# Gathered rows split into down and up halves, with five and seven places of their own, in a decoder layer with a product-key FFN

## The chip, the cores and the metric

The program runs on one core of a Trainium2 chip, in one launch. The metric is the device time of that core in microseconds. The engines are TensorE (PE), VectorE (DVE), ScalarE (ACT), GpSimd (POOL) and SyncE (SP, which only issues transfers); they run beside each other and meet at semaphores. Sixteen DMA engines move data between the chip's DRAM and the on-chip memory of 128 partitions.

## What is computed

One decoder layer on 1024 tokens of width 1024. A mixer (causal pooling, and spatial gating by chunks of 128 tokens) adds to x. Then each token picks 16 of 16,384 experts in each of 8 heads, and a weighted sum of the experts' rows adds to x again. The second part, cut down:

```python
q = (xb @ w_query).reshape(T, 8, 2, 128)
scores = jnp.einsum('thpd,hpkd->thpk', q, sub_keys)      # 128 keys each
s_top, i_top = lax.top_k(scores, 16)
cand = s_top[:, :, 0, :, None] + s_top[:, :, 1, None, :]
cand_idx = i_top[:, :, 0, :, None] * 128 + i_top[:, :, 1, None, :]
best, sel = lax.top_k(cand.reshape(T, 8, 256), 16)
idx = jnp.take_along_axis(cand_idx.reshape(T, 8, 256), sel, axis=-1)
gate = jax.nn.softmax(best, axis=-1)
u_e, v_e = expert_down[idx], expert_up[idx]              # 1024 floats each
act = jax.nn.gelu(jnp.einsum('thkd,td->thk', u_e, xb))
out = jnp.einsum('thk,thkd->td', gate * act, v_e)
```

So each of the 1024 tokens reads 128 down rows and 128 up rows of 4 KB, 1.07 GB in all, all in float32.

## The kernel before

The tokens are eight tiles of 128. The experts of a tile are served in 128 **slots**; slot g = 0 to 1023 runs over all tiles (`TABLE`, made by `slot_table`). A slot is one gather for 128 partitions, each with a token and one chosen expert: an indirect DMA that GpSimd issues, with a row of 8 KB for each partition from the table `experts`, in which an expert's down row and up row lie side by side. It moves 1 MB.

What happens to slot g, in this order:

- **L581**, POOL: the gather into place `x.ring`. Up to g = 267 there are 6 places of 8 KB (`RING_MIX`), from g = 268 (`LATE_SLOT`) 8. It waits until PE has used the row that was in the place before (`s_free`).
- **L1324**, DVE, `dot(x)`: waits for the row (`s_row`), multiplies the down half with the token's vector and sums it; the products overwrite the down half.
- **L950, L952, L957**, ACT, `expert_weight(x)`: gelu, times the gate, and a matrix `diag` of 128 x 32 that carries the weight.
- **L768**, PE, `add_expert(x)`: four matmuls (eight instructions in the trace, since float32 takes two passes) that add diag x up half into PSUM; the last one raises `s_free`.

Every engine has its program written out by hand as a loop over `TABLE`; after the work of slot g it does what else is due at g. The mixer of tile 1 to 7 is cut into 35 steps, and step n of tile t is due at slot `MIX_AT[t]` + n; the last is at slot 264. PE's share of these steps is the matmuls of L629, L640, L649, L659, L667 and L685. Routing (the choice of experts) for two heads at a time has its steps at `ROUTE_AT`: matmuls L737 and L750 on PE, 19 small steps on DVE. A slot's matmul therefore stands in PE's queue behind the mixer and routing matmuls of the slots before. Each engine works through its queue in order, and POOL issues slot g before slot g + 1.

Memory on chip is full. While the mixers run, `weights` holds w_in and w_out (20 units of 4 KB a partition), and `work` holds the 6 places, two buffers for the routing weights (`side_buf`) and the spread token vectors. After the last mixer step 16 routing blocks (`sides`, 576 KB each, 4.6 KB a partition) are loaded into `weights` for good, and two more places become free: one behind them, and one in `side_buf`. Before slot 0 two places hold the first routing blocks.

## Time and profile before

| | us |
|---|---|
| median of 3 runs | 2921.01 (2916.40 to 2921.32) |
| the profiled execution | 2921.73 |
| its span, first to last instruction | 2919.7 |

| engine | busy us | share of the span |
|---|---|---|
| PE matmul | 1976.8 | 68% |
| DVE | 1913.9 | 66% |
| ACT | 1210.3 | 41% |
| POOL | 1131.4 | 39% |

The DMA engines moved 1170.03 MB at a mean of 401 GB/s. The queue of the gathers alone held 147,456 packets and 1073.81 MB: 144 packets a gather, 128 rows and 16 that only signal. All other transfers are 93.84 MB. No compute engine is near its whole time, and the transfers are at 90% of it, so the table is to be read by stages: a stage has its own bound, and the mean over all hides it.

### The profile page before, as it was taken

How to read it: one execution, taken by the hardware profiler on the slowest of the kernel's cores; microseconds unless marked ns; L12 is line 12 of the kernel's file. 1: busy time of each engine (PE TensorE's matmuls, PEld its weight loads, DVE VectorE, ACT ScalarE, POOL GpSimd, SP SyncE). 2: the span in 40 equal slices, each digit the busy share in tenths (PEclk: the TensorE clock that was granted, in tenths of full speed). 3: DMA queues.
4: the chain of work that ended last, by engine and by line, in shares of the span. 5: the costliest groups of instructions: out<-in, count | busy, mean ns of one | idle time of the engine just before them, and what ended most of it. 6: DMA issues, size and time to landing. Idle time of an engine off the chain costs nothing.

```text
span 2919.7 us, 37542 instructions
## 1 busy us (share of the span) xinstructions
PE 1976.8 (68%) x12772; PEld 903.1 (31%) x12772; DVE 1913.9 (66%) x4710; ACT 1210.3 (41%) x3859; POOL 1131.4 (39%) x1032
## 2 busy tenths in 40 slices
PE   5788887887878566666666666566666666666554
PEld 4454443543534222222222323232222223232110
DVE  4876757665766376667576766667576766666554
ACT  1245444354544244444344444444344444444333
POOL 0044334344333344444444444444444444444332
PEclk9889988989889556666666656666666656565555
DMA  9599999999999999999999999999999999999997
GB/s 405 203 366 400 371 381 401 378 420 375 420 420 380 418 378 421 421 409 421 421 421 421 408 417 421 420 407 420 421 418 416 409 410 419 421 401 420 420 421 312
DMA packets 173396, 1170.03 MB, mean 401 GB/s; under 512 B 19475, under 2 KB 28691, under 8 KB 39958
## 3 DMA queue, kind: packets, MB, share of 16 engines
q0 software_dynamic: 147456, 1073.81, 89.9%
q1 hardware_dynamic: 25750, 93.84, 8.2%
q8 instruction: 101, 1.65, 0.2%
q14 instruction: 89, 0.73, 0.1%
HBM read 1159.18 MB, written 8.39 MB: 400 GB/s over the span
## 4 chain that ended last, share of the span: by engine, by line
DMA 50%; PE 24%; DVE 12%; ACT 7%; issue 3%; SPq 2%; POOL 1%; DVEq 0%; POOLq 0%; ACTq 0%
DMA work<-experts,expert_rows 42%; PE ps_sum L768 8%; DMA weights<-experts,expert_rows 6%; DVE work L1324 5%; PE ps_small L737 4%; PE ps_m L685 4%; PE ps_wide L711 3%; PE ps_m L649 2%; ACT diag L957 2%; PE ps_m L629 2%; ACT weight L952 2%; DMA out<-h_next 1%; SPq L543 1%; ACT act_out L950 1%; PE ps_m L640 1%
## 5 line engine op out<-in xcount | busy, mean ns | idle before, releaser
L581 POOL DMA_INDIRECT work<-experts,expert_rows x930 | 1027.6, 1105 | 1618.8 <-PE ps_sum L768 1438.2
L1324 DVE CUSTOM_DVE_ANT_0 work<-work 128x1024 f32<-128x1024 f32 x930 | 1134.5, 1222 | 720.1 <-DMA work<-experts,expert_rows 718.5
L768 PE MATMUL ps_sum<-work,diag 128*32 128x256 f32 x7440 | 837.4, 535 | 769.6 <-ACT diag L957 766.3
L950 ACT ACTIVATE act_out<-act_in 128x1 f32<-128x1 f32 x1024 | 207.5, 203 | 1189.4 <-DVE act_in L1324 1186.4
L768 PEld LDWEIGHTS ps_sum<-work,diag 128*32 128x32 f32 x7440 | 171.9, 127 | 1301.3 <-ACT diag L957 1228.1
L957 ACT ACTIVATE diag<-const,weight 128x32 f32<-128x32 f32 x1024 | 329.1, 321 | 33.5
L952 ACT ACTIVATE weight<-gate,act_out 128x1 f32<-128x1 f32 x1024 | 301.6, 295 | 33.2
L737 PE MATMUL ps_small<-h_t,weights 128*128 128x128 f32 x1344 | 299.5, 392 | 0.0
L737 PEld LDWEIGHTS ps_small<-h_t,weights 128*128 128x128 f32 x1344 | 257.0, 286 | 132.3 <-issue 125.0
L711 PE MATMUL ps_wide<-h_cur,const 32*128 32x512 f32 x260 | 209.4, 896 | 0.8 <-ACT work L924 0.8
L768 PE MATMUL ps_sum<-weights,diag 128*32 128x256 f32 x752 | 88.4, 557 | 108.0 <-ACT diag L957 100.9
L1324 DVE CUSTOM_DVE_ANT_0 weights<-weights,work 128x1024 f32<-128x1024 f32 x94 | 115.0, 1224 | 70.5 <-DMA weights<-experts,expert_rows 70.4
L581 POOL DMA_INDIRECT weights<-experts,expert_rows x94 | 100.8, 1072 | 142.3 <-PE ps_sum L768 140.4
L924 ACT COPY work<-ps_wide 128x512 f32<-128x512 f32 x144 | 83.6, 581 | 133.4 <-PE ps_wide L711 125.6
L685 PE MATMUL ps_m<-weights,h_buf 128*128 128x512 f32 x256 | 126.6, 621 | 0.7 <-DVE h_buf L1193 0.7
L737 PE MATMUL ps_small<-h_t,work 128*128 128x128 f32 x640 | 101.7, 310 | 0.9 <-ACT wide L937 0.9
L737 PEld LDWEIGHTS ps_small<-h_t,work 128*128 128x128 f32 x640 | 91.3, 218 | 35.3 <-issue 34.0
L931 ACT COPY q_t<-ps_small 128x128 f32<-128x128 f32 x124 | 32.4, 261 | 138.2 <-PE ps_small L737 137.4
L1324 DVE DVE_READ_ACCUMULATOR2_ANT act_in<- 128x1 f32 x1024 | 83.6, 82 | 0.0
L711 PEld LDWEIGHTS ps_wide<-h_cur,const 32*128 32x128 f32 x260 | 52.2, 249 | 82.3 <-issue 80.4
L950 ACT ACT_TABLE_LOAD x59 | 75.7, 1283 | 2.8 <-DVE act_in L1324 1.8
L649 PE MATMUL ps_m<-h_t,weights 128*128 128x128 f32 x512 | 76.2, 297 | 0.0
(161 smaller groups left out, 1665.8 us busy)
## 6 DMA issues: line engine op xcount, KB each, us to landing
work<-sides SPq DMA_DIRECT2D x44, 576.0 KB, 8.1
work<-w_ada SPq DMA_DIRECT2D x12, 2048.0 KB, 23.5
work<-experts,expert_rows POOLq DMA_INDIRECT x930, 16.2
weights<-sides SPq DMA_DIRECT2D x16, 576.0 KB, 37.2
weights<-w_in SPq DMA_DIRECT2D x3, 2048.0 KB, 17.5
x_buf<-x SPq DMA_DIRECT2D x8, 512.0 KB, 11.2
weights<-w_out SPq DMA_DIRECT2D x2, 2048.0 KB, 35.9
x_scratch<-h_buf SPq DMA_DIRECT2D x8, 512.0 KB, 8.1
```

The costliest lines, as they stand in the source:

```text
L581: nc.gpsimd.indirect_dma_start(ring[x.ring], None, experts, bass.IndirectOffsetOnAxis(ap=rows_flat[:, x.column:x.column + 1], axis=0),).th ...
L629: last = nc.tensor.matmul(ps_v[:, :], h_t[:, k, :], w_in_sb[:, 0, k, :], start=(k == 0), stop=(k == KC - 1))
L649: last = nc.tensor.matmul(ps_u[:, g * P:(g + 1) * P], w_in_sb[:, 2, k, g * P:(g + 1) * P], h_t[:, k, :], start=(k == 0), stop=(k == KC - 1))
L685: last = nc.tensor.matmul(ps_out[half], mixed_t[:, k, :], w_out_sb[:, k, half * HALF:(half + 1) * HALF], start=(part == 0 and i == 0), sto ...
L711: nc.tensor.matmul(ps_wide[:, :], quads[quarter(group), :], source[quarter(group), half * HALF:(half + 1) * HALF], start=True, stop=True). ...
L737: last = nc.tensor.matmul(ps_query(n), w_q[:, k, :], h2_t[:, k, :], start=(k == 0), stop=(k == KC - 1))
L768: last = nc.tensor.matmul(ps_sum[quarter(c), x.group, :], diag[:, x.ring, :], ring[x.ring][:, D + c * QCOLS:D + (c + 1) * QCOLS], start=x. ...
L924: nc.scalar.copy(h2_spread[k % 2][:, half * HALF:(half + 1) * HALF], ps_wide[:, :]).then_inc(s_wide_sb, 1)
L950: nc.scalar.activation(act_out[:, s:s + 1], act_in[:, s:s + 1], ACT.Gelu).then_inc(s_gelu, 1)
L952: nc.scalar.mul(weight[:, s:s + 1], gate_flat[:, x.column:x.column + 1], act_out[:, s:s + 1]).then_inc(s_weight, 1)
L957: nc.scalar.mul(diag[:, x.ring, :], quad_rows, weight[:, s:s + 1]).then_inc(s_diag, 1)
L1324: nc.vector.tensor_tensor_reduce(down, down, h2_spread[x.segment % 2], 1.0, 0.0, ALU.mult, ALU.add, act_in[:, x.g % TURN:x.g % TURN + 1]). ...
```

## The change

Up to slot 267 a slot is two gathers in place of one: 4 KB a partition from a table `downs`, and 4 KB from a table `ups`. Both tables are further inputs. The 12 half places of the six old places are the same memory (`UP_PLACES`, `DOWN_PLACES`), now five for down rows and seven for up rows. A down place is free when the dot of its last row is done (`s_dots`), an up place when PE has used its last row (`s_free`). POOL issues down g, up g, down g + 1 and so on. The dot waits for the down row alone; PE's product waits for the up row too. From slot 268 on whole rows go from `experts` into eight pairs of places, as before. `diag` has eight matrices throughout, no longer numbered by the ring. `weights` and `work` become parts of one tensor, `arena`.

```diff
 
 
-RING_MIX = 6
-RING = 8
+
+
+UP_PLACES = (20, 21, 22, 23, 24, 25, 26)
+DOWN_PLACES = (27, 31, 28, 29, 30)
+LATE_PAIRS = (18, 32, 20, 22, 24, 26, 28, 30)
+ALL_PLACES = range(18, 34)
+FIRST_SIDE_PLACE, SIDE_PLACE = 28, 32
+DIAGS = 8
 MIX_TILES = 2
 LATE_SLOT = 268
-LATE_ORDER = (6, 7, 4, 5, 0, 1, 2, 3)
 
 
...
         self.tile, self.s = g // SLOTS, g % SLOTS
-        self.ring = g % RING_MIX if g < LATE_SLOT else LATE_ORDER[g % RING]
-        self.fill, self.before = 0, None
+        self.up = self.down = self.up_before = self.down_before = None
+        self.down_fill = self.up_fill = 0
+        self.diag, self.whole = g % DIAGS, False
         self.first = self.last = self.opens = False
 
...
                         table.append(x)
-    fills, last = [0] * RING, [None] * RING
+    fills = dict.fromkeys(ALL_PLACES, 0)
+    last = {place: None for place in ALL_PLACES}
+
+    def longest_free(choices, halves):
+        def last_use(place):
+            return max(-1 if last[place + i] is None else last[place + i][1] for i in range(halves))
+        return min(choices, key=last_use)
+
     for x in table:
-        fills[x.ring] += 1
-        x.fill, x.before = fills[x.ring], last[x.ring]
-        last[x.ring] = x.g
+        x.whole = x.g >= LATE_SLOT
+        if x.whole:
+            x.down = longest_free(LATE_PAIRS, 2)
+            x.up = x.down + 1
+        else:
+            x.down, x.up = longest_free(DOWN_PLACES, 1), longest_free(UP_PLACES, 1)
+        x.down_before, x.up_before = last[x.down], last[x.up]
+        last[x.down], last[x.up] = ("free" if x.whole else "dot", x.g), ("free", x.g)
+        for place in {x.down, x.up} if not x.whole else {x.down}:
+            fills[place] += 1
+        x.down_fill, x.up_fill = fills[x.down], fills[x.up]
     return table, starts
 
 
 TABLE, SEGMENTS = slot_table()
 
 
-FIRST_SIDES = {2: 4, 3: 5}
+FIRST_SIDES = (2, 3)
 
...
 
-        weights = sb("weights", [P, KC * (IN_WIDTH + D)])
+        arena = sb("arena", [P, KC * (IN_WIDTH + D) + 12 * D + 2 * SIDE + 2 * D])
+        weights = arena[:, 0:KC * (IN_WIDTH + D)]
+        places = arena[:, 0:36 * D].rearrange("p (h n) -> p h n", n=D)
         w_in_sb = weights[:, 0:KC * IN_WIDTH].rearrange("p (b k n) -> p b k n", b=3, k=KC)
         w_out_sb = weights[:, KC * IN_WIDTH:].rearrange("p (k n) -> p k n", k=KC)
...
+
+        work = arena[:, KC * (IN_WIDTH + D):]
         ada_stage = [work[:, i * KC * D:(i + 1) * KC * D].rearrange("p (k n) -> p k n", k=KC) for i in range(2)]
-        ring = [work[:, r * 2 * D:(r + 1) * 2 * D] for r in range(RING_MIX)]
-        at_sides = RING_MIX * 2 * D
-        ring += [weights[:, SIDES * SIDE:SIDES * SIDE + 2 * D], work[:, at_sides:at_sides + 2 * D]]
-        side_buf = [work[:, at_sides + i * SIDE:at_sides + (i + 1) * SIDE] for i in range(2)]
-        at_spread = at_sides + 2 * SIDE
+        first_side_buf = {b: arena[:, FIRST_SIDE_PLACE * D + i * SIDE:FIRST_SIDE_PLACE * D + (i + 1) * SIDE]
+                          for i, b in enumerate(FIRST_SIDES)}
+        at_sides = SIDE_PLACE * D
+        side_buf = [arena[:, at_sides + i * SIDE:at_sides + (i + 1) * SIDE] for i in range(2)]
+        at_spread = 12 * D + 2 * SIDE
         h2_spread = [work[:, at_spread + i * D:at_spread + (i + 1) * D] for i in range(2)]
 
...
@@ -567,21 +591,33 @@
             for row in (gate1, shift2, scale2):
                 nc.gpsimd.memset(row[:, :], 0.0).then_inc(s_zero, 1)
             pool.wait_ge(s_acc, N_MOD * KC)
+
+            def both_places(x):
+                return arena[:, x.down * D:(x.down + 2) * D]
+
+            def wait_free(place, before):
+
+                if before is not None:
+                    pool.wait_ge(s_dots if before[0] == "dot" else s_free, before[1] + 1)
+                elif place >= SIDE_PLACE:
+                    pool.wait_ge(s_score, 4 * HELD_FROM)
+                elif FIRST_SIDE_PLACE <= place < FIRST_SIDE_PLACE + 3:
+                    pool.wait_ge(s_score, 4)
+
             for x in TABLE:
                 if x.opens:
                     pool.wait_ge(s_placed, x.tile * PAIRS + x.batch[-1] + 1)
                 if x.g == LATE_SLOT:
                     pool.wait_ge(s_o, TILES)
-                if x.before is not None:
-                    pool.wait_ge(s_free, x.before + 1)
-                elif x.ring == RING - 1:
-                    pool.wait_ge(s_score, 4 * HELD_FROM)
-                elif x.ring in FIRST_SIDES.values():
-                    pool.wait_ge(s_score, 4)
-                nc.gpsimd.indirect_dma_start(
-                    ring[x.ring], None, experts,
-                    bass.IndirectOffsetOnAxis(ap=rows_flat[:, x.column:x.column + 1], axis=0),
-                ).then_inc(s_row[x.ring], 16)
+                offset = bass.IndirectOffsetOnAxis(ap=rows_flat[:, x.column:x.column + 1], axis=0)
+                wait_free(x.down, x.down_before)
+                if x.whole:
+                    wait_free(x.up, x.up_before)
+                    nc.gpsimd.indirect_dma_start(both_places(x), None, experts, offset).then_inc(s_row[x.down], 16)
+                    continue
+                nc.gpsimd.indirect_dma_start(places[:, x.down, :], None, downs, offset).then_inc(s_row[x.down], 16)
+                wait_free(x.up, x.up_before)
+                nc.gpsimd.indirect_dma_start(places[:, x.up, :], None, ups, offset).then_inc(s_row[x.up], 16)
 
 
...
@@ -764,9 +800,11 @@
                 if x.g == 0:
                     pe.wait_ge(s_gate2, 1)
                 pe.wait_ge(s_diag, x.g + 1)
+                if not x.whole:
+                    pe.wait_ge(s_row[x.up], 16 * x.up_fill)
                 for c in range(QUADS):
-                    last = nc.tensor.matmul(ps_sum[quarter(c), x.group, :], diag[:, x.ring, :],
-                                            ring[x.ring][:, D + c * QCOLS:D + (c + 1) * QCOLS],
+                    last = nc.tensor.matmul(ps_sum[quarter(c), x.group, :], diag[:, x.diag, :],
+                                            places[:, x.up, c * QCOLS:(c + 1) * QCOLS],
                                             start=x.first, stop=x.last, skip_group_check=True)
                 last.then_inc(s_free, 1)
...
@@ -952,9 +990,9 @@
                 nc.scalar.mul(weight[:, s:s + 1], gate_flat[:, x.column:x.column + 1],
                               act_out[:, s:s + 1]).then_inc(s_weight, 1)
                 act.wait_ge(s_weight, x.g + 1)
-                if x.before is not None:
-                    act.wait_ge(s_free, x.before + 1)
-                nc.scalar.mul(diag[:, x.ring, :], quad_rows, weight[:, s:s + 1]).then_inc(s_diag, 1)
+                if x.g >= DIAGS:
+                    act.wait_ge(s_free, x.g - DIAGS + 1)
+                nc.scalar.mul(diag[:, x.diag, :], quad_rows, weight[:, s:s + 1]).then_inc(s_diag, 1)
 
             def square3(n):
...
@@ -1317,10 +1355,10 @@
                 nc.vector.tensor_copy(gate[:, :, columns], moved[:, 1, :, :]).then_inc(s_wide_sb, 1)
 
             def dot(x):
-                dve.wait_ge(s_row[x.ring], 16 * x.fill)
+                dve.wait_ge(s_row[x.down], 16 * x.down_fill)
                 if x.g == SEGMENTS[x.segment][0]:
                     dve.wait_ge(s_wide_sb, WIDE_USE["copy", x.segment, 1] + 1)
-                down = ring[x.ring][:, 0:D]
+                down = places[:, x.down, :]
                 nc.vector.tensor_tensor_reduce(down, down, h2_spread[x.segment % 2], 1.0, 0.0, ALU.mult, ALU.add,
                                                act_in[:, x.g % TURN:x.g % TURN + 1]).then_inc(s_dots, 1)
...
         "experts": np.concatenate([np.asarray(expert_down)[0], np.asarray(expert_up)[0]], axis=1),
+        "downs": rows(np.asarray(expert_down)[0]), "ups": rows(np.asarray(expert_up)[0]),
         "g_final": rows(g_final).reshape(-1),
         "constants": shape_constants(), "first_constants": first_tile_constants(),
```

On **GpSimd**, before slot 0 and the slots behind it, the kernel before:

```order
L581 DMA work<-experts,expert_rows 128x2048 [waits choices_placed,ada_sum_steps]
L581 DMA work<-experts,expert_rows 128x2048 x3
L581 DMA work<-experts,expert_rows 128x2048 [waits side_score_psum_ready] x2
L581 DMA work<-experts,expert_rows 128x2048 [waits ring_slots_used] x26
L581 DMA work<-experts,expert_rows 128x2048 [waits ring_slots_used,choices_placed]
```

and the changed one, from slot 4 to slot 7 (`dots_ready` is `s_dots`, `ring_slots_used` is `s_free`):

```order
L618 DMA arena<-downs,expert_rows 128x1024 [waits side_score_psum_ready]
L620 DMA arena<-ups,expert_rows 128x1024
L618 DMA arena<-downs,expert_rows 128x1024 [waits dots_ready]
L620 DMA arena<-ups,expert_rows 128x1024
L618 DMA arena<-downs,expert_rows 128x1024 [waits dots_ready]
L620 DMA arena<-ups,expert_rows 128x1024
L618 DMA arena<-downs,expert_rows 128x1024 [waits dots_ready]
L620 DMA arena<-ups,expert_rows 128x1024 [waits ring_slots_used]
```

Slot 6 was the first to wait for PE; now down 5 is the first that waits for a dot, and up 7 the first that waits for PE. In all 268 instructions more stand in this queue.

On **PE**, in the mixer of tile 1 (L649 is a projection of the mixer, L659 the spatial product; L685 and L695 are their numbers after), the kernel before:

```order
L659 MATMUL ps_m<-w_sp_t,vn_u 128x128 x3
L768 MATMUL ps_sum<-work,diag 32x256 [waits diags_ready]
L768 MATMUL ps_sum<-work,diag 32x256 x3
L649 MATMUL ps_m<-h_t,weights 128x128 x4
L768 MATMUL ps_sum<-work,diag 32x256 [waits diags_ready]
```

and the changed one:

```order
L695 MATMUL ps_m<-w_sp_t,vn_u 128x128 x3
L806 MATMUL ps_sum<-arena,diag 32x256 [waits rows_in_place26_landed,diags_ready]
L806 MATMUL ps_sum<-arena,diag 32x256 x3
L685 MATMUL ps_m<-h_t,arena 128x128 x4
L806 MATMUL ps_sum<-arena,diag 32x256 [waits rows_in_place20_landed,diags_ready]
```

Nothing moved on PE; the first matmul of a product waits for one more semaphore. The other engines' queues keep their order.

## Rows read from the trace of the kernel before

**Rows 1.** Stages: length, busy us of each engine (instructions), PE clock, DMA share, GB/s

```profile
148.00:944.00 796.00, 655.24 (x4372) 351.53 (x4371) 536.12 (x1408) 370.50 (x1107) 308.89 (x269) 0.88 0.99 393
944.00:1040.00 96.00, 43.37 (x250) 20.25 (x250) 38.69 (x79) 27.43 (x84) 26.77 (x26) 0.55 0.97 398
1040.00:2900.00 1860.00, 1179.14 (x7698) 466.00 (x7698) 1236.82 (x3049) 779.47 (x2593) 792.73 (x729) 0.62 1.01 416
```

**Rows 2.** The same view: a late stretch, and two saturated ones among the mixers

```profile
1110.00:1280.00 170.00, 111.80 (x732) 48.20 (x732) 114.28 (x286) 68.84 (x236) 72.90 (x68) 0.64 1.01 421
...
590.00:660.00 70.00, 57.72 (x380) 30.76 (x378) 46.39 (x127) 40.21 (x114) 29.09 (x24) 0.83 1.02 420
740.00:870.00 130.00, 106.16 (x718) 53.53 (x715) 93.00 (x257) 62.30 (x189) 52.24 (x48) 0.88 1.01 420
```

**Rows 3.** The same view: six stretches in which PE is nearly always busy

```profile
210.00:230.00 20.00, 20.00 (x96) 8.51 (x96) 6.63 (x14) 6.58 (x23) 6.28 (x6) 0.95 0.90 340
330.00:360.00 30.00, 28.39 (x152) 12.41 (x151) 17.62 (x43) 11.67 (x37) 10.03 (x9) 0.97 0.90 323
400.00:440.00 40.00, 36.81 (x291) 26.28 (x292) 24.05 (x61) 18.00 (x51) 13.87 (x12) 0.96 0.93 346
530.00:550.00 20.00, 19.74 (x170) 13.65 (x169) 8.79 (x13) 6.84 (x24) 8.46 (x7) 1.00 0.85 329
690.00:720.00 30.00, 28.58 (x174) 13.01 (x173) 14.52 (x26) 10.40 (x39) 12.02 (x10) 1.00 0.93 343
870.00:900.00 30.00, 29.07 (x261) 21.85 (x260) 14.77 (x29) 13.85 (x43) 11.99 (x11) 1.00 0.97 376
```

**Rows 4.** Line L581, 148 to 944 us: issues, POOL's waits, who waits for them

```profile
L581 POOL DMA_INDIRECT work<-experts,expert_rows x269: 933/938/2529, 148.1 to 940.1; - x135
...
  PE ps_sum L768: 473.8, 247
...
  DVE work L1324: 149.1, 112
```

**Rows 5.** Timeline at 412 us: start, us, engine, line, operation, idle time before

```profile
412.16 1.22 DVE L1324 CUSTOM_DVE_ANT_0 work<-work 128x1024 f32<-128x1024 f32 x1
413.41 1.22 DVE L1324 CUSTOM_DVE_ANT_0 work<-work 128x1024 f32<-128x1024 f32 x1
419.89 0.64 PE L768 MATMUL ps_sum<-work,diag 128*32 128x256 f32 x8
420.83 0.94 POOL L581 DMA_INDIRECT work<-experts,expert_rows  x1 [2.86 <-PE ps_sum L768]
428.65 1.23 DVE L1324 CUSTOM_DVE_ANT_0 work<-work 128x1024 f32<-128x1024 f32 x1 [2.66 <-DMA work<-experts,expert_rows]
```

**Rows 6.** Timeline of POOL: three of the first six issues

```profile
148.07 1.08 POOL L581 DMA_INDIRECT work<-experts,expert_rows  x1 [144.52 <-DVE expert_rows L1316]
149.46 0.94 POOL L581 DMA_INDIRECT work<-experts,expert_rows  x1 [0.30 <-issue]
...
151.94 0.93 POOL L581 DMA_INDIRECT work<-experts,expert_rows  x1 [0.31 <-issue]
```

**Rows 7.** Timeline at 339 us: a dot and two issues

```profile
339.22 1.23 DVE L1324 CUSTOM_DVE_ANT_0 work<-work 128x1024 f32<-128x1024 f32 x1 [0.97 <-DMA work<-experts,expert_rows]
...
339.27 1.99 POOL L581 DMA_INDIRECT work<-experts,expert_rows  x1 [3.27 <-PE ps_sum L768]
...
341.56 1.05 POOL L581 DMA_INDIRECT work<-experts,expert_rows  x1 [0.30 <-issue]
```

**Rows 8.** Stretches: 16 KB rows; 16 side loads beside gathers; single loads beside gathers

```profile
30.00:62.00 32.00, 23.44 (x114) 17.00 (x114) 14.58 (x21) 3.23 (x10) 0.00 (x0) 0.95 1.01 431
...
950.00:970.00 20.00, 6.53 (x45) 2.21 (x46) 10.71 (x23) 6.89 (x18) 9.37 (x10) 0.50 1.02 419
...
720.00:730.00 10.00, 4.43 (x37) 2.12 (x36) 3.34 (x5) 1.79 (x7) 4.45 (x5) 0.88 1.02 428
```

**Rows 9.** Line L768, 148 to 944 us: what ended PE's idle time before it

```profile
  ACT diag L957: 337.6, 199
```

More of the change, by code:

```diff
@@ L392, in build @@
         s_h2c = sem("h2_cur_ready")
-        s_row = [sem(f"expert_row{r}_landed") for r in range(RING)]
+        s_row = {place: sem(f"rows_in_place{place}_landed") for place in ALL_PLACES}
         s_free = sem("ring_slots_used")
@@ L520, in _ @@
             for b in range(2, 4):
[L521 removed]
+                sp.dma_start(first_side_buf[b], sides[b]).then_inc(s_side0, 16)
             load_x(1)
```

8 lines of the change are left out of this document (3 added, 5 removed).

## The prediction

> **What bounds the kernel now.** I read the table of stages first, because one share over the whole span hides two different kernels [rows 1]. Up to 148 us nothing is gathered. From 1040 us to 2900 us the DMA engines move 416 GB/s at a share of 1.01: they are the bound there, and the change leaves that part's transfers as they are. Between 148 and 944 us, while the mixers run, they move only 393 GB/s. The 796 us at 393 GB/s are 312.8 MB; at the 421 GB/s of an undisturbed late stretch [rows 2] they would take 743 us. So 53 us is all that this stage could give back if nothing else moved. That stage holds the 268 gathers that the change splits: the first starts at 148.07 us [rows 6], the 269th at 940.1 us [rows 4], so a row now takes (940.1 - 148.1) / 268 = 2.96 us.
>
> Where are the 53 us? The second table of stretches shows six in which PE is busy 92 to 100% of the time and the DMA falls to 323 to 376 GB/s [rows 3]. Against 421 GB/s they lose 20 x 81 + 30 x 98 + 40 x 75 + 20 x 92 + 30 x 78 + 30 x 45 = 13,090, over 421: 31 us. In the saturated stretches between them the rate is 420 GB/s and there is nothing to gain [rows 2]. The rest of the 53 us is spread thin, part of it in transfers with 1 KB rows.
>
> Who holds the gathers up there? GpSimd (POOL) issues them, and in this stage it waits 473.8 us, 247 times, for PE's expert product L768, which empties a place [rows 4]. One loop of such a stretch stands in [rows 5]: PE ends the product at 419.89 + 0.64 = 420.53 us, POOL issues into the emptied place at 420.83 us, and that row's dot on VectorE starts at 428.65 us, after 2.66 us of idle time put down to the DMA. The product itself is late because PE has mixer matmuls in front of it, not because its row is late: the dot that ended at 412.16 + 1.22 = 413.38 us belongs to the product of 420.53 us, 7 us later [rows 5]. So a place of 8 KB is held until PE has used its upper half, though its lower half was done with at the dot.
>
> **The change part by part.** *Places.* The same 12 half places are now five for down rows and seven for up rows. An up gather waits for the product seven rows back in place of six. In the stretches of [rows 3] POOL issued 6, 9, 12, 7, 10 and 11 gathers in 170 us: 3.1 us each, so up halves can start some 3.1 us earlier. A down gather waits for the dot five rows back. For the gather issued at 420.83 us that is, counted back in the trace, the dot at 413.41 us; it ended at 414.63 us, 6 us before the product that really released the gather [rows 5]. But POOL issues in order, and the down gather stands behind the up gather of the row before, which waits for a product eight rows back, one whole row earlier still; so the down half can use most of those 6 us. Taking 3.1 us for the one half and about 5 us for the other, a stretch starts with 4 us more of transfers done or queued. Six stretches: 6 x 4 = **24 us gained**. The floor of this term is the up half alone over the whole row, less what stretches too short to drain the queue don't need, about 12 us; its ceiling is the 31 us above.
>
> *Where it does not help.* In 148 to 200 us and after the bursts of the routing steps VectorE is late itself; there the dot five rows back comes up to 1 us after the product six rows back. The down half goes 1 us later and the up half stands behind it, but the dot no longer waits for the whole 8 KB row. I take these as even, 0 us.
>
> *GpSimd.* It issues 268 instructions more, and each down-up pair costs two. One takes 0.94 us with 0.30 us between two that wait for nothing [rows 6], so a pair takes at least 2 x 1.24 = 2.48 us. The mean in this stage is 308.89 / 269 = 1.15 us [rows 1], which makes 2 x 1.45 = 2.90 us. The lengthening has a cause that rows show: the issue at 339.27 us took 1.99 us, with a dot running from 339.22 to 340.45 us, and the next, 0.18 us before another dot, took 1.05 us [rows 7]; the first issues of all, beside no dot, took 0.93 to 0.94 us four times in six [rows 6]. So an issue that starts inside a dot waits for the dot's end and takes 0.8 us from there. A pair at 2.90 us is below the 2.96 us of a row, but in the fastest saturated stretch, 740 to 870 us, POOL issued 48 rows in 130 us, 2.71 us each [rows 2]. There 0.19 x 48 = 9 us would be lost; at 2.48 us nothing. I take **5 us lost**; the ends are 0 and 9 us, and what happens above 2.96 us is a rival below. The cover of those issues is POOL's idle time, 792 - 309 = 483 us now; after, about 170 us.
>
> *Packets.* A row is now two packets of 4 KB in place of one of 8 KB. No gather of 4 KB rows is in this trace, so bounds. At the start, loads with 16 KB rows run at 431 GB/s, the late gathers with 8 KB rows at 421 GB/s [rows 8, 2]. An engine (one of 16) thus takes 608 ns for 16 KB in one packet and 2 x 311.3 = 622.6 ns in two: 14 ns for a further packet. Eight rows an engine: 0.115 us for a gather, 268 of them 31 us; only the 622 us outside the six stretches count, 24 us. On the other side, where 16 loads with 4.6 KB rows run beside gathers, the rate is 419 GB/s, and with single loads of 4 to 4.6 KB rows 428 GB/s [rows 8], no lower than without: 0 us. These are nearer to the new case in row size, but they ran on a second queue, so I don't take their 0 alone: **10 us lost**, between 0 and 24 us.
>
> The page "DMA: Bandwidth & Descriptors" of the Trainium skill, section "Rules for kernel authors", wants at least 1 MiB in a DMA for full bandwidth, which speaks against gathers of 0.5 MiB. Its section "Measured (HBM→SBUF, 128 partitions, SWDGE, issued from GpSimd)" gives some 10.5 ns a packet; as an estimate from that page 144 more packets over 16 engines are 0.095 us a gather, or 25 us over 268. Its 1 MiB was measured for a transfer alone, and no run here shows one alone.
>
> *The rest.* PE waits for one more semaphore before a product (the up half's landing). Both halves are issued 1.2 us or so apart, and between them lie the dot, three operations on ScalarE and PE's queue, so the up half is there first: 0 us, unless POOL runs late, which is then the same loss as above. The eight small matrices of ScalarE (in place of six) never hold it: 0 us. From row 268 on whole rows go into eight pairs as before. The stage of 944 to 1040 us follows PE's last mixer step and keeps its length; it only moves with the end of this stage.
>
> **Sum.** 24 - 5 - 10 = 9 us, off the profiled run's 2921.7 us (span 2919.7 us), and off the median of 2921.0 us, from which it differs by 0.7 us: about 2912 us.
>
> **The rivals.** *Slower: GpSimd becomes the bound.* Down gathers are now released by a dot's end, and where rows have already landed the next dot starts at once (412.16 and 413.41 us in [rows 5] are such followers). An issue some 0.3 us behind a dot's end then falls into the next dot and waits about 0.8 us more. If that lifts the mean to more than 1.18 us, a pair takes more than 2.96 us, and POOL sets the pace: that is the deciding point. At 1.21 us, a pair of 3.02 us, the stage takes 268 x 3.02 = 809 us in place of 792: 17 us more, 2938 us. At 1.25 us it would be 3.10 us, 831 us, and 2960 us; an issue time above that in the mean would need nearly every second issue to start in a dot. For it: after a stall POOL can't catch up any more, at 2.48 us against 1.24 us a row. Against it: issues that followed each other without a wait took no longer than others, 0.94 us mostly at the start and 1.05 us behind one that had been locked [rows 6, 7], since an issue held to a dot's end leaves the next one clear of it. The price I take is 2938 us.
>
> *No change: the packets eat the gain.* With the full 24 us for packets, or half the gain in the stretches, the sum lies between +5 and -5 us: 2916 to 2926 us. The saturated stretches are 622 of the 792 us, which speaks for it.
>
> *The stretches are PE's own.* If PE's work alone set their length, earlier rows would not shorten them. But PE waits 337.6 us in this stage for ScalarE's small matrix before a product [rows 9], and the dots wait 149.1 us for rows [rows 4], so the loop comes back to it. This would end as the case of no change or, with the costs, at 2921 + 15 = 2936 us.
>
> **How the numbers follow.** Faster, as in the sum: 0.45, at 2912 us, between 2888 and 2915 us (the gain of 31 us with no cost at the low end). No change: 0.21. Slower, by GpSimd or by packets without the gain: 0.34, most of it between 2927 and 2945 us. A measurement of this kernel can tell about 0.2%, or 6 us, from no change. The range of 2888 to 2945 us leaves out the far end of POOL's rival and little below: 2 in 10 at most.
>
> **What would show it.** The stage of 148 us to the 269th row should end near 931 us (792 - 9 us). POOL's mean issue should stay at 1.15 us or below; its wait for PE should shrink to well under 200 us, with a new wait for the dots. Stretches with PE above 92% should show 380 GB/s or more. Packets: saturated stretches in this stage at 402 GB/s (8 KB in 311.3 + 14.4 ns an engine) would be the full cost, 420 none. From 1040 us on the rate should be 416 GB/s as before. I would be wrong if POOL shows hardly any wait (it is the bound), or if the stretches keep 340 GB/s with rows already landed (PE's own work).

## The result, and the profile after

The changed kernel took 3002.3 us (median of four runs, 2993.8 to 3016.4) against 2918.7 us for the kernel before: a ratio of 1.0294, 95% interval 1.0273 to 1.0315. It is 2.9% slower where 0.3% faster was forecast. The profiled run took 2994.88 us, its span is 2993.0 us.

The stages of the changed kernel, columns as in [rows 1], with the stretches of [rows 2] and [rows 3] behind them:

```profile
148.00:944.00 796.00, 617.93 (x3940) 330.59 (x3940) 491.18 (x1295) 341.26 (x1013) 554.52 (x496) 0.84 0.96 362
210.00:230.00 20.00, 17.54 (x75) 7.70 (x73) 6.69 (x13) 4.29 (x17) 13.90 (x14) 0.93 1.02 401
330.00:360.00 30.00, 23.08 (x120) 10.81 (x120) 27.97 (x83) 9.35 (x32) 18.01 (x17) 0.72 0.83 298
...
740.00:870.00 130.00, 103.03 (x681) 56.78 (x680) 72.29 (x179) 52.79 (x167) 89.16 (x84) 0.88 0.98 376
1110.00:1280.00 170.00, 108.92 (x761) 43.75 (x764) 123.77 (x333) 73.98 (x250) 75.71 (x71) 0.68 0.99 409
1040.00:2900.00 1860.00, 1176.88 (x7670) 474.26 (x7670) 1225.02 (x3032) 768.49 (x2556) 749.43 (x718) 0.62 1.01 415
```

The late part is what it was (415 GB/s). The whole loss is in the stage of the mixers: 362 GB/s in place of 393, and 376 in a stretch that was saturated at 420 [rows 2]. PE and VectorE are less busy there than before, so neither became the bound. The line of the down gathers, and GpSimd (POOL) at the end of the stage:

```profile
L618 POOL DMA_INDIRECT arena<-downs,expert_rows x268: 932/941/1990, 147.3 to 1009.3; - x134
...
  DVE act_in L1362: 69.8, 22
1011.78 0.94 POOL L616 DMA_INDIRECT arena<-experts,expert_rows  x1 [0.30 <-issue]
```

The first whole row goes at 1011.78 us, so 268 rows took 1011.78 - 147.3 = 864.5 us where they took 792: 72.5 of the 73.3 us between the spans of the two traces (2993.0 and 2919.7 us) are here. POOL's mean issue is 1.12 us, as hoped, and it still waits 70 us for dots and, on its other line, 34 us for PE. A look at what ScalarE (ACT) waited for gives the first hint:

```profile
ACT act_out L988 <- DVE act_in L1362: 143.9, 70, 11.4
...
ACT q_t L969 <- remote: 47.4, 8, 10.3
ACT act_out L988 <- issue: 41.0, 20, 5.5
ACT arena L962 <- remote: 26.6, 5, 10.5
```

"remote" and "issue" mean that the trace names no instruction that ended the wait. In the kernel before neither stands once on PE, VectorE or ScalarE in this stage. The two are not the same thing. "remote": the semaphore's update is in the trace, but no instruction ended near it. "issue": the update is not in the trace at all. The 20 waits of L988 put down to "issue" are ordinary ones whose record is missing: ScalarE starts less than 0.1 us after VectorE's dot ends in every one of them.

### The profile page after: what moved, and what is told of

It is laid out like the page before. It is cut to its first block, busy times and chain, and to the rows that moved or that the text cites. A ratio compares the mean times of both kernels' runs of the same rounds, so it can differ in the third digit from the quotient of the medians.

```text
span 2993.0 us, 38818 instructions
## 1 busy us (share of the span) xinstructions
PE 1995.4 (67%) x12772; PEld 912.2 (30%) x12772; DVE 1912.2 (64%) x4710; ACT 1208.1 (40%) x3859; POOL 1393.4 (47%) x1300
## 4 chain that ended last, share of the span: by engine, by line
DMA 46%; PE 20%; DVE 11%; issue 8%; ACT 7%; another core or an unknown queue 3%; POOL 3%; SPq 2%; POOLq 0%; DVEq 0%; ACTq 0%
DMA arena<-experts,expert_rows 41%; PE ps_sum L806 7%; DVE arena L1362 6%; PE ps_small L773 4%; DMA arena<-downs,expert_rows 3%; PE ps_m L721 2%; PE ps_wide L747 2%; ACT diag L995 2%; ACT weight L990 1%; PE ps_m L685 1%; DMA out<-h_next 1%; POOL arena L620 1%; PE ps_m L665 1%; SPq L567 1%
## 5 line engine op out<-in xcount | busy, mean ns | idle before, releaser
L1362 DVE CUSTOM_DVE_ANT_0 arena<-arena 128x1024 f32<-128x1024 f32 x1024 | 1248.1, 1222 | 759.5 <-DMA arena<-experts,expert_rows 632.2
L806 PE MATMUL ps_sum<-arena,diag 128*32 128x256 f32 x8192 | 932.9, 540 | 912.2 <-ACT diag L995 833.8
L616 POOL DMA_INDIRECT arena<-experts,expert_rows x756 | 789.9, 1045 | 1165.5 <-PE ps_sum L806 1110.2
L988 ACT ACTIVATE act_out<-act_in 128x1 f32<-128x1 f32 x1024 | 207.4, 203 | 1157.2 <-DVE act_in L1362 1109.3
L806 PEld LDWEIGHTS ps_sum<-arena,diag 128*32 128x32 f32 x8192 | 190.7, 128 | 1500.2 <-ACT diag L995 1320.8
L618 POOL DMA_INDIRECT arena<-downs,expert_rows x268 | 299.2, 1116 | 290.1 <-DVE expert_rows L1354 143.7
L773 PE MATMUL ps_small<-h_t,arena 128*128 128x128 f32 x1984 | 402.3, 365 | 5.4 <-issue 4.3
L773 PEld LDWEIGHTS ps_small<-h_t,arena 128*128 128x128 f32 x1984 | 348.0, 263 | 172.8 <-issue 163.4
L620 POOL DMA_INDIRECT arena<-ups,expert_rows x268 | 301.2, 1124 | 117.4 <-issue 65.8
L962 ACT COPY arena<-ps_wide 128x512 f32<-128x512 f32 x144 | 83.9, 582 | 161.4 <-PE ps_wide L747 113.3
L721 PE MATMUL ps_m<-arena,h_buf 128*128 128x512 f32 x256 | 128.8, 631 | 1.7 <-issue 1.0
L969 ACT COPY q_t<-ps_small 128x128 f32<-128x128 f32 x124 | 32.6, 263 | 182.2 <-PE ps_small L773 120.6
L685 PE MATMUL ps_m<-h_t,arena 128*128 128x128 f32 x512 | 80.3, 307 | 0.0
L685 PEld LDWEIGHTS ps_m<-h_t,arena 128*128 128x128 f32 x512 | 68.8, 210 | 25.7 <-issue 25.7
L676 PE MATMUL ps_m<-h_t,arena 128*128 128x128 f32 x512 | 71.2, 295 | 4.7 <-issue 4.7
```

What stands on the lines that cost most here:

```text
L616: nc.gpsimd.indirect_dma_start(both_places(x), None, experts, offset).then_inc(s_row[x.down], 16)
L618: nc.gpsimd.indirect_dma_start(places[:, x.down, :], None, downs, offset).then_inc(s_row[x.down], 16)
L620: nc.gpsimd.indirect_dma_start(places[:, x.up, :], None, ups, offset).then_inc(s_row[x.up], 16)
L685: last = nc.tensor.matmul(ps_u[:, g * P:(g + 1) * P], w_in_sb[:, 2, k, g * P:(g + 1) * P], h_t[:, k, :], start=(k == 0), stop=(k == KC - 1))
L721: last = nc.tensor.matmul(ps_out[half], mixed_t[:, k, :], w_out_sb[:, k, half * HALF:(half + 1) * HALF], start=(part == 0 and i == 0), sto ...
L773: last = nc.tensor.matmul(ps_query(n), w_q[:, k, :], h2_t[:, k, :], start=(k == 0), stop=(k == KC - 1))
```

## What the engines do in such a wait

Of the experiments below one is needed at once: the same program on another chip took 2927.9 us. The two traces can be laid side by side, row by row. The first down gathers start 0.7 us apart, the 26th 1.9 us and the 29th 6.6 us. ScalarE and PE of the changed kernel as first measured (start, length, engine, line, operation, idle time before):

```profile
217.47 0.32 ACT L995 ACTIVATE diag<-const,weight 128x32 f32<-128x32 f32 x1
...
218.24 0.32 ACT L995 ACTIVATE diag<-const,weight 128x32 f32<-128x32 f32 x1
229.05 0.59 ACT L962 COPY arena<-ps_wide 128x512 f32<-128x512 f32 x1 [10.49 <-remote]
...
222.11 1.12 PE L747 MATMUL ps_wide<-h_cur,const 32*128 32x512 f32 x2
...
224.25 0.95 PE L806 MATMUL ps_sum<-arena,diag 128*32 128x256 f32 x4
226.00 0.38 PE L806 MATMUL ps_sum<-arena,diag 128*32 128x256 f32 x1 [0.80 <-issue]
226.72 0.41 PE L806 MATMUL ps_sum<-arena,diag 128*32 128x256 f32 x2 [0.35 <-issue]
227.42 0.38 PE L806 MATMUL ps_sum<-arena,diag 128*32 128x256 f32 x1 [0.29 <-issue]
228.82 3.31 PE L721 MATMUL ps_m<-arena,h_buf 128*128 128x512 f32 x4 [1.02 <-issue]
```

And the same place on the other chip:

```profile
220.84 1.12 PE L747 MATMUL ps_wide<-h_cur,const 32*128 32x512 f32 x2
...
222.97 0.64 PE L806 MATMUL ps_sum<-arena,diag 128*32 128x256 f32 x8
...
222.05 0.58 ACT L962 COPY arena<-ps_wide 128x512 f32<-128x512 f32 x1 [4.71 <-PE ps_wide L747]
```

There ScalarE copies PE's result 0.09 us after it is done (220.84 + 1.12 = 221.96). Here PE is done at 223.23 us and the copy starts at 229.05, 5.8 us late, and a product (eight matmul instructions), which waits for nothing after its first, takes from 224.25 to 227.80 us in place of 0.64. Behind the copy stand the mixer, the dots and the places. I call this a late start.

The name says where it is seen, not where it arises. The trace also keeps the time of each semaphore update: the one that this copy waits for, raised by PE, is recorded at 228.97 us, 0.08 us before the copy and 5.7 us after the matmul. All 38 "remote" waits of over 0.3 us on ScalarE, VectorE and GpSimd in this stage are like it: the semaphore is one that PE raises, its update comes 1.6 us or more after PE's instruction ended (up to 7.5 us where ScalarE or VectorE waits), and the waiting engine starts within 0.4 us of the update. ScalarE and VectorE are never over 0.1 us late behind each other; only PE, behind ScalarE's matrix, is late too, over 1 us in five places. In alternate (an experiment below, on another such chip) both engines wait for the same matmul, and go on at the same moment, 2.15 us after it:

```profile
905.48 1.16 PE L685 MATMUL ps_m<-h_t,arena 128*128 128x128 f32 x8
...
908.79 0.59 ACT L937 COPY vn_u<-ps_m 128x512 f32<-128x512 f32 x1 [2.72 <-remote]
...
908.79 0.76 DVE L1145 TENSOR_TENSOR h_t<-a_t 128x572 f32<-128x572 f32 x1 [7.03 <-remote]
```

So it is the signal from PE that comes late, not the engine that waits for it. Whether the matmul itself ended later can't be told, since the ends of matmuls in a trace are modelled.

Late starts can be counted: from the timelines of both engines I took, for 148 to 940 us, each of ScalarE's two kinds of copy of a PE result (L962 and L969; L924 and L931 before) for which ScalarE stood idle, and its start less PE's end (or less the start of the idle time, if later). The median is 0.09 us in all of these rows but no_lock's (0.31 us). The last column is something else. A gather's landing raises its semaphore 16 times, and the recorder should keep each time; the column is the share of these records that the whole trace lacks.

| kernel, chip | copies | over 1 us | sum of delays, us | ratio to before | records missing |
|---|---|---|---|---|---|
| before | 67 | 0 | 4.5 | 1 | none |
| changed, chip of the result | 61 | 16 | 58.6 | 1.0294 | 20% |
| changed, chip 14 | 66 | 0 | 4.6 | 1.0036 | 0.1% |
| changed, chip 5 | 65 | 16 | 52.1 | 1.0274 | 20% |
| no_lock, chip 13 | 65 | 22 | 76.4 | 1.0367 | 22% |
| two_six, chip 13 | 67 | 11 | 38.4 | 1.0148 | 18% |
| alternate, chip 13 | 67 | 0 | 4.4 | 1.0021 | 7% |
| filler2, chip 13 | 68 | 0 | 4.6 | 1.0006 | 2.7% |
| filler3, chip 5 | 66 | 0 | 4.5 | 1.0042 | 2.7% |
| tiny128, chip 9 | 68 | 0 | 4.6 | 1.0060 | 0.1% |
| tiny16, chip 9 | 67 | 0 | 4.5 | 1.0026 | 0.3% |
| tiny128, chip 1 | 66 | 7 | 18.6 | 1.0133 | 20% |

The records go missing where the time goes: in the changed kernel as first measured the trace holds 9 of 16 a gather from 160 to 940 us, and 15.6 of 16 from 1100 to 2800 us.

## The experiments

The kernels ran in six groups, each on one chip (the expectations say "call" for a group), and the kernel before ran again in each: its median was 2918.5 to 2920.5 us on every chip.

**First group, chip 13.** Four kernels on the theories of the prediction. GpSimd's time alone, in the kernel before (`filler` is 128 x 400):

```
+                if x.g < LATE_SLOT:
+                    for k in range(2):
+                        pool.wait_ge(s_filler, 2 * x.g + k)
+                        nc.gpsimd.memset(filler[:, :], 0.0).then_inc(s_filler, 1)
```

> The kernel before, unchanged but for two small memsets (128 x 400) on GpSimd behind each of the first 268 gathers: GpSimd gets about as much to do a slot as the two gathers of the changed kernel give it (2.84 us there: 2 x 1.12 + 2 x 0.30), while rows stay 8 KB in one packet and the six places stay as they are. Theory A (GpSimd's time a slot is what costs the changed kernel its 74 us, since it can't catch up after a wait): the stage up to slot 268 grows by 40 to 90 us, to 830 to 880 us, and GpSimd's wait for PE shrinks from 474 us to under 120 us. Rival B (the 4 KB packets cost it, GpSimd only looks busy): no change, 2915 to 2930 us in all. Rival C (down places released too late): no change either.

2918.3 us, ratio 1.0006 (0.9995 to 1.0016). POOL is busy 558 us of the stage's 796 and the kernel is as fast: theory A falls at this dose, and the time is as rivals B and C had it.

Six and six places, both held until PE's product:

```
-UP_PLACES = (20, 21, 22, 23, 24, 25, 26)
-DOWN_PLACES = (27, 31, 28, 29, 30)
+UP_PLACES = (20, 21, 22, 23, 24, 25)
+DOWN_PLACES = (26, 27, 31, 28, 29, 30)
-        last[x.down], last[x.up] = ("free" if x.whole else "dot", x.g), ("free", x.g)
+        last[x.down], last[x.up] = ("free", x.g), ("free", x.g)
```

> The changed kernel with six places for down and six for up halves, both released by PE's product as in the kernel before: two gathers a slot and nothing of the new release. Theory A: as slow as the changed kernel or slower, 2990 to 3030 us, since the cost is in the second issue. Rival B: the same. Rival C (five down places, released by dots, hold GpSimd up): faster than the changed kernel by the 70 us that GpSimd waits for dots there, 2920 to 2945 us.

2964.3 us, 1.0148 (1.0132 to 1.0165): half of the loss without any of the change's own places, and in neither of the two ranges.

Every second row whole (`x.whole = x.g >= LATE_SLOT or x.g % 2 == 0`), in six pairs of places:

> Only the odd slots up to 267 are two gathers of 4 KB rows, the even ones one gather of 8 KB rows; six pairs of places, all released by PE's product. GpSimd has 1.5 issues a slot, 1.5 x 1.42 = 2.13 us, well under the 2.96 us a slot takes in the kernel before; half of the additional packets stay. Theory A: most of the loss is gone, 2915 to 2940 us. Rival B: a cost by packets is linear in them, so about half of the loss stays, 2950 to 2965 us.

2925.1 us, 1.0021 (1.0011 to 1.0030). With 134 rows split in place of 268 nearly nothing is lost, as theory A had it. None of the counted copies is late, but this is the trace of the late signal shown above, at 908.79 us.

The changed kernel without the dots' hold on GpSimd:

```
+                if x.g < LATE_SLOT:
+                    nc.vector.tensor_reduce(act_in[:, x.g % TURN:x.g % TURN + 1], down, AX_X, ALU.add).then_inc(s_dots, 1)
+                    return
```

> The changed kernel with the dots of slots 0 to 267 replaced by a plain sum of the down row, one SBUF input in place of two (the product with the token's vector is left out of the computation there). Theory A with issues lengthened by dots: GpSimd's mean issue falls from 1.12 us to 0.95 to 1.0 us, a pair from 2.84 us to 2.5 to 2.6 us, and the stage of 864 us shortens by 50 to 80 us, to 2915 to 2945 us in all. If the sum locks GpSimd as well, or if the lengthening is not what matters: 2980 to 3000 us.

3024.9 us, 1.0367 (1.0350 to 1.0384). This felled the theory that GpSimd's held issues cost the time: POOL was freer (436 us busy from 148 to 900 us, where the changed kernel has 520) and the kernel slower still, outside both ranges.

**Second group, chip 7.** Parts of the places, and a larger dose of GpSimd's time:

> The changed kernel with one place moved: six for down halves, released by the dot, and six for up halves, released by PE. So far: two gathers a slot with six and six, all released by PE, gave 2964 us; the changed kernel with five and seven 3002 us. Theory D (five down places are too few: a down place is held until VectorE has done the dot, and VectorE is often held up by PE's mixer and routing results, while GpSimd can't pass the waiting down gather): 2950 to 2968 us, and GpSimd's wait for dots falls from 70 us to under 25 us. Rival E (the release by the dot itself, or the order of releases, costs it, not the number): stays at 2990 to 3005 us.

2918.9 us, 1.0000 (0.9987 to 1.0012); this is six and six places with the down place released by the dot. It is far below both ranges.

> The changed kernel with its seventh up place left unused: five down, six up places. Theory D: the up places hardly matter once five down places hold GpSimd up: within 8 us of the changed kernel, 2995 to 3012 us. If the additional up place does bring what the forecast gave it (3 us for each of six stretches): 3015 to 3025 us.

2928.9 us, 1.0034 (1.0021 to 1.0047); the edit is `UP_PLACES = (20, 21, 22, 23, 24, 25)`. It is below both ranges too.

> The kernel before with three memsets (128 x 480) on GpSimd behind each of the first 268 gathers, 2.85 to 2.9 us of GpSimd's time a slot, as the two gathers take; two memsets (2.25 us a slot) had cost nothing. Theory A, mended (GpSimd's time costs only where it comes near the 2.96 us that a slot takes): 2950 to 2975 us, like two gathers with six places. Rival B (packets of 4 KB cost the 45 us of that kernel): 2915 to 2930 us.

2929.8 us, 1.0040 (1.0025 to 1.0054), with three memsets of 128 x 480: below theory A's range, at the top of rival B's.

> Two gathers a slot, six places for each half, all released by PE, and the dots of slots 0 to 267 replaced by a plain sum of the down row (the product with the token's vector is left out of the computation there). GpSimd's issue falls from 1.14 us to about 0.97 us as in the changed kernel with the plain sum. Theory A, mended: a pair takes 2.54 us in place of 2.87 us, so most of the 45 us goes: 2920 to 2945 us. Rival B: 2955 to 2970 us, as with the dots.

2921.1 us, 1.0010 (0.9999 to 1.0022); two_six with the plain-sum dots of no_lock: in theory A's range, though two_six itself turned out at 2927 us on such a chip.

None was near 2960. Either the places explained it all, or this chip was another matter. So the next groups repeated known programs.

**Third group, chip 14.**

> The changed kernel again, on one chip with six-and-six kernels. The two calls before gave results that don't fit together: six and six released by PE 2964 us in one call, six and six with down released by the dot 2919 us and five and six 2929 us in the other. If the kernels differ: about 3000 us again, since it was 2994 to 3016 us in four runs. If the chips differ (the calls ran on two chips) and this is the one of the second call or one like it: 2920 to 2940 us.

2927.9 us, 1.0036 (1.0022 to 1.0050).

> Six and six, all released by PE's product, again, beside the changed kernel. If the kernels differ: 2958 to 2966 us as in the first call. If the chips differ: within 0.5% of the kernel before wherever the changed kernel is too.

2926.9 us, 1.0034 (1.0022 to 1.0046), where the first group had 2964.

> Six and six with down places released by the dot, again, on the same chip as the two above. If the kernels differ: 2915 to 2925 us as in the second call. If the chips differ and this one is like the first call's: between 2950 and 2970 us, near two_six_again.

2920.5 us, 1.0010 (1.0000 to 1.0020).

The same program loses 0.4% or 2.9%, and it is the traces with unexplained waits that are the slow ones.

**Fourth group, chip 5.** Is it the chip?

> The changed kernel once more. Theory: in its slower runs the engines lose time between one engine's end and the next engine's start (a copy of ScalarE after TensorE's last matmul: 0.1 us where the kernel before runs, 2 to 6 us in 16 of 61 cases of the slower run), and whether this happens depends on the chip and not on the program. Then the time is either 2994 to 3016 us with such gaps, or 2924 to 2934 us without any; nothing between. Rival: the order of the work around the halves' places costs the time on every chip, by the luck of a start; then one call gives times spread over both.

3003.0 us, 1.0274 (1.0257 to 1.0291), all four runs between 2998 and 3007.

> The changed kernel whose dot products of the first 268 rows are plain sums of the down half (that part of the computation is left out), once more; it took 3024.9 us where the changed kernel took 3002. Theory: if the changed kernel takes 2928 in this call, this one takes 2915 to 2930, since its GpSimd is held less (plain-sum dots with six and six places: 2921); if that takes 3000, this one takes 3010 to 3030. Rival, that plain sums or the earlier issue themselves cost the time: 3000 or more in any call.

3028.3 us, 1.0373 (1.0356 to 1.0391).

> Six and six places, both released by TensorE's product, once more. Theory: 2920 to 2930 us where the changed kernel takes 2928, and about 2960 where that takes 3000. Rival, the places alone decide: 2964 as first measured, in any call.

2961.8 us, 1.0136 (1.0119 to 1.0152).

> The kernel before with three memsets of GpSimd, 128 by 480, behind each of its first 268 gathers, once more, beside the changed kernel on one chip. Its packets, places and gathers are those of the kernel before. Theory: 2926 to 2934 us in any call, since what it adds is GpSimd's time alone (0.4%), and no gap between the engines; the changed kernel's loss where it takes 2928 us is of this same size. Rival, that GpSimd's time itself makes the gaps between engines: then it is slow where the changed kernel is, by 1% or more.

2931.2 us, 1.0042 (1.0025 to 1.0058), as on chip 7.

All three split kernels are slow together, no_lock and two_six by about the amounts of chip 13. The rival of a lucky order falls. filler3's 0.4% is the same on both sorts of chip, and none of the counted copies in its trace is late.

**Fifth and sixth group, chips 9 and 1.** Which part of the change brings the late starts on? In the kernel before, behind each of the first 268 gathers a second one of short pieces that nobody reads (`{n}` is 128 or 16):

```
+                    nc.gpsimd.indirect_dma_start(
+                        tiny_rows[0:{n}, x.g % 8, :], None, tiny,
+                        bass.IndirectOffsetOnAxis(ap=rows_flat[0:{n}, x.column:x.column + 1], axis=0),
+                    ).then_inc(s_tiny[x.g % 8], 16)
```

> The kernel before, with a second gather of 128 short pieces (64 bytes, of a table of their own, into a tile that nobody reads) behind each of its first 268 gathers: GpSimd issues and DMA packets as many as in the changed kernel, whole rows and places as before, bytes nearly as before. On a chip where the changed kernel takes 3000 us: if the number of gathers or of packets makes the engines start late (ScalarE's copies 2 to 6 us after TensorE's last matmul), this one is 1% or more slower and shows such gaps; if it needs the changed kernel's halves and places, it takes 2920 to 2932 us (GpSimd's time as in the kernel with three memsets) and shows none. On a chip where the changed kernel takes 2928: 2920 to 2932 either way.

2935.3 us, 1.0060 (1.0043 to 1.0077), chip 9, above the 2932 us expected of such a chip.

> The same with 16 pieces of 64 bytes in the second gather: as many gathers and completions as in the changed kernel, but 16 packets in place of 128 for the second. On a slow chip: if the number of gathers makes the gaps, 1% or more slower like its neighbour with 128; if the number of packets does, 2918 to 2930 us and no gaps. On a fast chip 2918 to 2930 either way.

2926.8 us, 1.0026 (1.0015 to 1.0036), chip 9. Neither trace has a late start, so this group could not tell. It did price a second gather: 0.26% with 16 pieces, 0.60% with 128. The two don't differ in packets, as the expectations had it: both traces count 156,032 packets of gathers, 32 more a row than before (16 of data, 16 that signal), since the 128 pieces moved as 16 packets of 512 bytes. Of the 8.5 us between them, 5 us are an estimate for the 2 MB more (at 421 GB/s); an issue also takes 0.95 us in place of 0.85.

> The kernel before with a second gather of 128 short pieces behind each of its first 268 gathers, once more. On a chip of the kind where the changed kernel takes 3000 us (seen by waits that nothing explains on ScalarE, VectorE and TensorE): if the number of gathers and packets makes the late starts, 2950 us or more with such gaps of 1 us and more between TensorE's end and ScalarE's copy; if halves and places are needed, 2930 to 2940 us as first measured, without. On a chip of the other kind 2930 to 2940 us either way.

2957.8 us, 1.0133 (1.0116 to 1.0150), chip 1, with 7 late starts. What ScalarE and PE waited for:

```profile
ACT act_out L959 <- issue: 41.9, 24, 6.4
ACT q_t L940 <- remote: 11.7, 4, 4.4
...
PE ps_sum L777 <- issue: 35.5, 21, 4.2
```

The first line is again ordinary waits whose records are missing: none of the 24 starts over 0.1 us after the dot. So is most of the last: all starts of PE behind ScalarE's matrix together are 7 us late. The late starts are the second line and 7 of the copies in the table. So late starts need neither halves nor their places, nor the 144 packets that a split adds to a row. A second gather behind each row is enough, on such a chip.

## Why the prediction was wrong

**What it lacked: 74 us.** Of the 84 us between 3002.3 and 2918.7 us, 9.5 are lost on chips without late starts as well (2927.9 - 2918.5). The other 74 come with the late starts, a mechanism in no term and no rival: "The rest", put at 0 us, took PE's results to reach the other engines as promptly as before. They come on chips 13, 5, 1 and that of the result, not on 7, 14 and 9. As measured they belong to the change all the same: the kernel before lost no time to them on any chip, not even with GpSimd as busy (filler3 on chip 5), and a second gather did (tiny128 on chip 1).

*What stays open.* Why PE's signals are late on such a chip isn't settled. It isn't just the count of gathers: changed, two_six, no_lock and tiny128 all have 268 more and lose 84, 45, 106 and 39 us; alternate with 134 more loses 6. The freer the issuing (plain-sum dots, seven up places), the more is lost. What these kernels share is a second issue by GpSimd and 16 more signals a row; which of the two counts can't be told.

A rival stands untested, and it is a strong one: the recorder itself. Each timed run has a granted clock on record, so the recorder ran in all of them. The kernels that lose 39 us and more are just those whose traces lack 18 to 22% of the gathers' records; with 7% missing 6 us are lost; with 2.7% filler3 loses what it loses on chip 7, and filler2 nothing. A recorder that can't keep up might hold PE, and the changed kernel would then lose only its 9.5 us when nothing is recorded; or one cause makes both. No run without it is on record, so the 74 us are what was measured, and not shown to be the kernel's own.

The Trainium skill, page "Runtime: NRT & Kernel Launch", section "Instruction fetch mechanics", says that each engine's instructions are brought in by its own DMA queue in 16 KiB blocks, mostly hidden. A late block might look like this, and packets of 8 or 16 KB of that kind do lie beside 5 of the 16 late copies, from 3 us before the wait to its end. Beside the other 11 there are none. In one of these ScalarE stands from 263.21 to 267.94 us, with PE's result done at 260.58, and from 262 to 268 us the DMA engines moved gathers only:

```profile
267.94 0.27 ACT L969 COPY q_t<-ps_small 128x128 f32<-128x128 f32 x1 [4.73 <-remote]
...
DMA packets 678, 2.47 MB, mean 411 GB/s; under 512 B 76, under 2 KB 76, under 8 KB 678
## 3 DMA queue, kind: packets, MB, share of 16 engines
q0 software_dynamic: 678, 2.47, 103.1%
```

So instruction blocks don't explain the 11.

**The sum, on a chip without late starts.** It said 9 us gained; measured are 9.5 lost. The changed kernel on chip 14:

```profile
148.00:944.00 796.00, 659.45 (x4348) 352.84 (x4346) 530.20 (x1388) 368.17 (x1100) 600.03 (x535) 0.86 1.01 390
210.00:230.00 20.00, 20.00 (x106) 8.72 (x106) 8.04 (x18) 5.59 (x20) 14.47 (x15) 1.00 1.03 411
330.00:360.00 30.00, 27.87 (x140) 13.04 (x140) 19.33 (x50) 12.00 (x38) 23.14 (x21) 0.90 0.98 369
400.00:440.00 40.00, 36.33 (x303) 25.59 (x301) 26.42 (x67) 18.58 (x52) 28.80 (x27) 1.00 1.02 403
530.00:550.00 20.00, 19.64 (x168) 13.49 (x167) 9.12 (x14) 8.51 (x31) 15.29 (x15) 1.00 1.03 409
690.00:720.00 30.00, 28.57 (x182) 13.20 (x181) 14.70 (x26) 10.40 (x39) 23.91 (x21) 1.00 0.97 363
870.00:900.00 30.00, 29.07 (x250) 20.83 (x247) 15.38 (x30) 13.03 (x40) 19.09 (x17) 1.00 1.00 393
590.00:660.00 70.00, 55.42 (x367) 29.34 (x367) 44.80 (x125) 37.78 (x107) 53.06 (x48) 0.83 1.03 408
740.00:870.00 130.00, 106.27 (x698) 52.74 (x690) 91.76 (x253) 63.26 (x190) 98.97 (x94) 0.83 1.03 409
...
  DVE act_in L1362: 37.7, 18
944.86 0.94 POOL L616 DMA_INDIRECT arena<-experts,expert_rows  x1 [0.30 <-issue]
```

- *Places, 24 us gained.* The six stretches did rise, from 344 GB/s in the mean of their 170 us to 390: (390 - 344) x 170 / 421 = 19 us. But filler3, with the places of before, has 372 GB/s in the same stretches (chip 5; 374 on chip 7): a stage whose issues are slower elsewhere has rows left to move there. So the rate in fixed stretches was a poor measure of what places give: at most the 18 GB/s over filler3, 7 us, is theirs. In the sum the step that failed is to count a fuller stretch as time won.
- *"Even, 0 us" where VectorE is late.* Mis-sized. The down gather waited 37.7 us for the dot five rows back, 18 times, up to 6.0 us at once. With a sixth down place (two_six_dot, chip 14) it waits 0.9 us, and the ratio is 1.0010 in place of 1.0036 on chip 14, and 1.0000 against five_six's 1.0034 on chip 7: 7 to 10 us for one place. The release by the dot is worth 6 us: two_six_dot against two_six, 2920.5 against 2926.9 us on chip 14.
- *Packets, 10 us lost.* Saturated stretches run at 408 and 409 GB/s in place of 420: 622 x (1 - 409 / 420) = 16 us, inside the 0 to 24, nearer its top. That is a rate, not time lost: two_six_dot has the same packets, 406 to 410 GB/s there, and loses 0 to 2 us in all. For 8 KB on each of 16 engines, 131,072 bytes, that is 320.5 ns at 409 GB/s against 312.1 ns at 420: 8.4 ns for a further packet; the estimate from the Trainium skill's page "DMA: Bandwidth & Descriptors", cited in the prediction, was 10.5 ns, and this trace is near it. (The page has it as 0.67 us for 64 packets, and doesn't say over how many engines; that each engine takes so long was the prediction's reading.)
- *GpSimd, 5 us lost, the deciding point at a pair of 2.96 us.* The pair came to 2 x (1.12 + 0.30) = 2.84 us, below the point, and yet it costs. filler3, with POOL's wait for PE down to 17 to 21 us from 473.8 [rows 4], loses 11 us; tiny16, with 66 us left, loses 8; filler2, with 199 us left, nothing. The changed kernel has 54 us left (37.7 for dots, 15.8 for PE). So the mean pace was the wrong test. What fits better is the slack left for catching up after each stall, which the rival's "for it" had named and its deciding point left out. Slack alone isn't the rule either: two_six_dot has 46 to 53 us left and loses 0 to 2 us. That held issues matter here is suggested by no_lock_six, 1.0010 against two_six's 1.0034, though the two ran on different chips.
- *Right:* the up half is in time (PE waited 8.4 us for it in the stage), POOL's mean issue is 1.12 us and its wait for PE far below 200 us, and the late part keeps its rate.

On such a chip the terms are thus 7 us gained, 16 us lost to packets, and GpSimd's 8 to 11 us. Taken in full they would make 17 to 20 us lost where 9.5 are measured, and more with the missing down place, so they overlap: a queue that is short of rows isn't slowed by packets and GpSimd twice. How they overlap is argued, not measured.

## What to carry to other kernels

An engine's mean pace below the pace of the work doesn't make it free: look at how much wait it has left to make up for stalls. Two memsets a row left GpSimd 199 us of it in 796 us and cost nothing; three left 17 to 21 us and cost 11 us. Don't take a higher rate in a fixed stretch for time won, unless a kernel that only shifts the work lacks it. When a profile can't explain a wait, lay the start beside the end of what it waits for: here many such waits were on time with a record missing, and the late ones pointed at PE. And before explaining a difference, run the same program on a second chip, and once without the recorder if you can: a kernel that splits its gathers lost 0.4% on one chip and 2.9% on another, while the kernel it is compared with was the same on all.

## What the runs showed of the hardware

- On some chips (three of the six whose numbers are known) the semaphore updates of TensorE's matmuls are recorded up to 10.8 us after the matmul's end (changed, chip 5), once GpSimd issues two gathers a row; ScalarE and VectorE behind each other start within 0.1 us. In the traces with one gather of a whole row at a time (filler2 on chip 13, filler3 on chip 5) none of the counted copies was late. The traces with late updates also lack 7 to 22% of the gathers' records, and no run tells which comes from which.
- A gather issued by GpSimd takes 0.94 us with 128 rows, 0.95 us with 128 pieces of 64 bytes and 0.85 us with 16 (median), so the pieces are a small part of it.
- A gather of 128 pieces of 64 bytes moved as 16 packets of 512 bytes, one a DMA engine (tiny128).
- Two packets of 4 KB take an engine 8 ns longer than one of 8 KB: 409 against 420 GB/s.
